# Two-layer YOCO trunk on one core: the spread of the sums of squares as two words, two of its places moved into a unit, and a cut of lower words around the last x tile

## What is computed

```python
h = h + 0.5 * swiglu(rmsnorm(h, ffn1_norm[l]), ffn1_w_gate_up[l], ffn1_w_down[l])
u = rmsnorm(h, mix_norm[l])
# layer 0: main = gated DeltaNet, projections u @ gdn_w_in; layer 1: main = forgetting attention
h = h + jnp.concatenate([main, mem_out], axis=-1) @ w_out[l]
h = h + 0.5 * swiglu(rmsnorm(h, ffn2_norm[l]), ffn2_w_gate_up[l], ffn2_w_down[l])
# after layer 0: shared_fox_kv(h) = rmsnorm(h, kv_norm) @ kv_w
```

```python
y = x32 * lax.rsqrt(jnp.mean(x32 * x32, axis=-1, keepdims=True) + EPS)   # then * gain
```

## Time and profile before

| | us |
|---|---|
| median of 3 runs (1984.55 to 1986.69) | 1986.46 |
| the profiled execution, own time | 1986.4 |
| its span, first to last instruction | 1984.7 |
| TensorE busy in it | 1959.9 |
| VectorE busy | 908.2 |
| ScalarE busy | 732.2 |
| GpSimd busy | 395.1 |

### The profile page before, as it was taken

The page is one execution under the profiler, slowest core; times in us unless marked ns, Lnnn a source line. Parts: engine busy times, 40 slices in busy tenths (PEclk is TensorE's granted clock), DMA queues, the critical chain, the costliest instruction groups (busy, mean ns, idle before and its releaser), DMA issues.

```text
span 1984.7 us, 24949 instructions
## 1 busy us (share of the span) xinstructions
PE 1959.9 (99%) x9755; PEld 1612.3 (81%) x9755; DVE 908.2 (46%) x898; ACT 732.2 (37%) x882; POOL 395.1 (20%) x274
## 2 busy tenths in 40 slices
PE   9999999999999999999999999999999999999997
PEld 7888888888777888888888888888887788888886
DVE  5544334378875543433334434343446553433323
ACT  5422222245445443432232434332235444433221
POOL 1312221113813321211110122121101041212111
PEclk9999999999999999999999999999999999999999
DMA  6243322354311333332334333323260133333232
GB/s 193 87 126 106 106 73 88 105 157 114 90 46 44 87 104 106 87 97 87 88 99 160 114 105 85 106 78 96 87 216 22 43 106 106 89 101 92 81 95 71
DMA packets 330145, 195.60 MB, mean 99 GB/s; under 512 B 18591, under 2 KB 326960, under 8 KB 329570
## 3 DMA queue, kind: packets, MB, share of 16 engines
q1 hardware_dynamic: 327248, 182.55, 32.1%
q10 hardware_dynamic: 1938, 9.00, 1.3%
q0 software_dynamic: 896, 3.16, 0.4%
HBM read 188.23 MB, written 6.46 MB: 98 GB/s over the span
## 4 chain that ended last, share of the span: by engine, by line
PE 92%; DVE 5%; ACT 2%; issue 1%; ACTq 0%; POOL 0%; DVEq 0%
PE ps L595 29%; PE ps L597 29%; PE ps L596 29%; DVE w_lo L1724 1%; DVE v L2029 1%; ACT w_hi L1269 1%; DVE q L2029 1%; PE ps L1162 1%; PE ps L1188 0%; PE ps L654 0%; PE ps L676 0%; PE ps L666 0%; PE ps L1173 0%; PE ps L903 0%; PE ps L883 0%
## 5 line engine op out<-in xcount | busy, mean ns | idle before, releaser
L595 PE MATMUL ps<-x_hi,w_hi 128*128 128x512 f32 x1792 | 707.2, 395 | 1.7 <-DVE w_lo L1724 1.6
L597 PE MATMUL ps<-x_hi,w_lo 128*128 128x512 f32 x1792 | 697.8, 389 | 0.0
L596 PE MATMUL ps<-x_lo,w_hi 128*128 128x512 f32 x1792 | 697.6, 389 | 0.0
L1269 ACT ACTIVATE w_hi<-raw 128x2048 fp32r<-128x2048 f32 (+1 forms) x186 | 320.5, 1723 | 755.7 <-PE ps L597 755.7
L1724 DVE TENSOR_TENSOR w_lo<-raw,w_hi 128x2048 fp32r<-128x2048 f32 (+1 forms) x186 | 405.9, 2182 | 208.2 <-ACT w_hi L1269 208.2
L595 PEld LDWEIGHTS ps<-x_hi,w_hi 128*128 128x128 f32 x1792 | 336.5, 188 | 76.1 <-issue 4.1
L597 PEld LDWEIGHTS ps<-x_hi,w_lo 128*128 128x128 f32 x1792 | 336.3, 188 | 70.6
L596 PEld LDWEIGHTS ps<-x_lo,w_hi 128*128 128x128 f32 x1792 | 336.6, 188 | 68.0 <-issue 1.0
L597 PE MATMUL ps<-hid_hi,w_lo 128*128 128x512 f32 x704 | 273.9, 389 | 0.0
L595 PE MATMUL ps<-hid_hi,w_hi 128*128 128x512 f32 x704 | 273.9, 389 | 0.0
L596 PE MATMUL ps<-hid_lo,w_hi 128*128 128x512 f32 x704 | 273.9, 389 | 0.0
(11 more groups left out here) (315 smaller groups left out, 1439.3 us busy)
## 6 DMA issues: line engine op xcount, KB each, us to landing
raw<-in_ffn_w_gate_up SPq DMA_DIRECT2D x174, 512.0 KB, 4.9
raw<-in_ffn_w_down SPq DMA_DIRECT2D x64, 384.0 KB, 4.0
raw<-in_ffn_w_down SPq DMA_DIRECT2D x64, 320.0 KB, 3.3
raw<-in_gdn_w_in SPq DMA_DIRECT2D x26, 512.0 KB, 4.8
raw<-in_w_out SPq DMA_DIRECT2D x16, 512.0 KB, 4.3
raw<-in_kv_w SPq DMA_DIRECT2D x12, 512.0 KB, 4.7
raw<-in_mem_w_kv SPq DMA_DIRECT2D x8, 512.0 KB, 4.2
raw<-in_fox_w_in SPq DMA_DIRECT2D x8, 512.0 KB, 4.5
```

Source lines behind the costliest of these rows:

```text
L595: nc.tensor.matmul(dst, hi, xh, start=first, stop=False)
L596: nc.tensor.matmul(dst, hi, xl, start=False, stop=False)
L597: return nc.tensor.matmul(dst, lo, xh, start=False, stop=last)
L1269: nc.scalar.activation(w_hi[s][:, 0:n], raw[s][:, 0:n], ACT.Copy).then_inc(hi_ready, 1)
```

## The change

Four edits.

1. `spread_sum` is two fp32r matmuls, ones by `sum_hi` and ones by `sum_lo`, in place of one float32 matmul. ScalarE makes `sum_hi` from `square_sum` (in `root_mean_square`, ahead of the wait for the spread), VectorE makes `sum_lo` (in `reciprocal_of_rms`, ahead of the wait for the root). The spread waits for both words (`sum_words`) and no longer for GpSimd's last add. The final phase calls the ScalarE helper too, so `sum_hi` is also made there, and nothing reads it.
2. In gdnin0 and kv0 the spread no longer stands between unit 0 and unit 1, but inside unit 1, behind its third x tile (`SPREAD_BESIDE = 2`), that is behind 18 of its 48 matmuls. In up1, foxin0 and up3 it stays between the units.
3. At the end of down0, down1 and down2 the lower words of the next phase's unit 1 are made in two halves, one ahead of the last `x_lo` and one behind it.
4. The two words of the sum take place in `gate_up`, in the half that holds the up outputs.

```diff
+SPREAD_BESIDE = 2
...
+        sum_hi = place("sum_hi", [P, SEQ], F32R, at=pair_at + 2048)
+        sum_lo = place("sum_lo", [P, SEQ], F32R, at=pair_at + 6144)
...
             def spread_sum(name, tokens=SEQ):
 
-                pe.wait_ge(sum_ready, KT * (sums_before[name] + 1))
-                nc.tensor.matmul(ps[:, 4, 0:tokens], ones[:], square_sum[:, 0:tokens],
-                                 start=True, stop=True).then_inc(sum_done, 1)
+                pe.wait_ge(sum_words, 2 * sums_before[name])
+                nc.tensor.matmul(ps[:, 4, 0:tokens], ones[:].bitcast(F32R), sum_hi[:, 0:tokens], start=True, stop=False)
+                nc.tensor.matmul(ps[:, 4, 0:tokens], ones[:].bitcast(F32R), sum_lo[:, 0:tokens],
+                                 start=False, stop=True).then_inc(sum_done, 1)
...
                     def beside(n, s):
 
+                        if n == 1 and s == SPREAD_BESIDE:
+                            spread_sum(fed_by[name])
...
                              beside=lambda c: beside(n, c))
-                        if n == 0:
-                            spread_sum(fed_by[name])
...
                 elif kind == "kv":
+                    def spread_beside(c):
+
+                        if c == SPREAD_BESIDE:
+                            spread_sum(fed_by[name])
+
                     for n in range(1 + HEADS):
...
-                             release=n == HEADS)
-                        if n == 0:
-                            spread_sum(fed_by[name])
+                             release=n == HEADS, beside=spread_beside if n == 1 else None)
...
             def root_mean_square(name, dst, tokens=SEQ):
+                act.wait_ge(sum_ready, KT * (sums_before[name] + 1))
+                nc.scalar.activation(sum_hi[:], square_sum[:], ACT.Copy).then_inc(sum_words, 1)
                 act.wait_ge(sum_done, sums_before[name] + 1)
...
             def reciprocal_of_rms(name, dst):
                 n = sums_before[name] + 1
+                dve.wait_ge(sum_words, 2 * sums_before[name] - 1)
+                nc.vector.tensor_tensor(sum_lo[:], square_sum[:], sum_hi[:].bitcast(F32), ALU.subtract).then_inc(sum_words, 1)
...
+                        if m == KT - 1 and name != last_update:
+                            cut_lo_part(u + 2 * m + 3, 0)
+                            feed_lo(name, x_lo[:, c:c + 1, :], h[:, c:c + 1, :],
+                                    gains[:, gain + c:gain + c + 1], x_hi[:, c:c + 1, :], m)
+                            cut_lo_part(u + 2 * m + 3, 1)
+                            return
```

More of the change, by code:

```diff
@@ L371, in build_trunk @@
         sq_ready, sum_zero, sum_ready = sem("sq_ready"), sem("sum_zero"), sem("sum_ready")
-        sum_done = sem("sum_done")
+        sum_done, sum_words = sem("sum_done"), sem("sum_words")
         rms_ready, rstd_ready = sem("rms_ready"), sem("rstd_ready")
```

## The result

| | before | changed |
|---|---|---|
| median, us | 1986.36 | 1993.13 |
| lowest to highest of 7 runs | 1984.55 to 1986.69 | 1991.37 to 1994.61 |
| profiled execution, own time | 1986.4 | 1991.37 |
| its span | 1984.7 | 1989.6 |

The ratio is 1.0034, with a 95% interval of 1.0025 to 1.0043: slower, by 6.8 us at the median and by 4.9 in the profiled executions' spans. The forecast was 1991.8, with a range from 1988.8 to 1994.3.

The account below looks back on a forecast made before the run. TensorE, busy 1959.9 of 1984.7 us, was taken to bound the kernel. The terms 4.7 + 1.5 - 0.4 - 0.2 - 0.2 = +5.4 us on the profiled 1986.4 gave 1991.8 us, range 1988.8 to 1994.3.

Parts of the forecast that it names:

- The delay of the root, 4.82: In gdnin0 and kv0, the spread inside unit 1 makes the root start 4.82 us later, with everything hanging on it.
- gdnin0 +4.7: In gdnin0, TensorE waits 1.6 us ahead of unit 2 and 2.9 ahead of unit 3; phase 4.7 us late.
- the 0.28 us of slack ahead of unit 3: In gdnin0, unit 3's lower words are ready only 0.28 us before TensorE needs them: all the chain's slack.
- The first rival: Waits inside VectorE's and ScalarE's chain are slack and swallow the root's delay: 1985.5 us; chance 10%.
- kv0 +1.5: In kv0, unit 2 starts 1.4 us later, plus 0.1 for starting again; no wait ahead of unit 3.
- foxin0 -0.4: In foxin0, the words have time, so the cheaper spread gains 0.4 us.
- up3 -0.2: In up3, the words come late as in up1, leaving a gain of 0.2 us.
- up1 -0.2: In up1, a 0.15 us wait for late words and 0.05 restart cut the spread's 0.40 us gain to 0.2.
- The final phase, 0: In the final phase, the copy and table load fit into ScalarE's 4.31 us wait for products, costing 0.
- From there late by the same amount, and I count no more: After gdnin0's unit 3, TensorE and VectorE stay late by the same amount; nothing further counted.
- the third rival: The clock falls in gdnin0's new 2.9 us wait, costing 2.3 us more: 1994.1 us; chance 10%.
- the second rival: Later in gdnin0, TensorE's 2.7 us of waits for turned values shrink, giving back loss: 1989.1 us; chance 13%.

Follow-up runs that it names:

- experiment 5: Changed kernel with the spread behind the first x tile of unit 1 in place of the third: 1987.43 us, ratio 1.0006.
- experiment 6: Changed kernel with the spread behind the second x tile of unit 1 in place of the third: 1990.68 us, ratio 1.0022.
- experiment 12: Changed kernel with the spread behind the fifth x tile of unit 1 in place of the third: 1999.38 us, ratio 1.0066.
- experiment 7: Changed kernel with unit 1's banks emptied and unit 3's lower words made earlier in gdnin0's gate chain: 1989.98 us, ratio 1.0018.
- experiment 8: Changed kernel with two words only in up1, foxin0 and up3, float32 spread between units in gdnin0 and kv0, halves kept: 1986.24 us, ratio 0.9999.
- experiment 3: Kernel before with only unit 1's lower words made in two halves around the last x_lo: 1986.70 us, ratio 0.9998.
- experiment 11: Changed kernel with the spread back between the units in gdnin0 alone: 1988.24 us, ratio 1.0007.
- experiment 10: Changed kernel measured and profiled a second time, no edit: 1991.38 us, ratio 1.0029.
- experiment 9: Kernel before with two words in up1, foxin0 and up3, and gdnin0's first query scaling behind the third v_tok copy: 1985.25 us, ratio 0.9994.

## Why the prediction was right

**The delay of the root, 4.82: measured 4.76.** It was built from the place of the 18th matmul, the end of the halves and the length of two matmuls. The halves ended at 404.19 + 2.31 = 406.50, less the offset of 0.25 at 406.25, predicted 406.3: the second half took 2.31 us where the first took 1.23, so the add did cost 1.1, as assumed.

**gdnin0 +4.7: measured 4.5** at unit 3's start (433.54 - 428.77 - 0.25). The two waits are 1.47 and 2.68, predicted 1.6 and 2.9. The whole step rested on the 0.28 us of slack ahead of unit 3, and on reading the 3.36 us ahead of the gate step as part of the chain. Both held: the chain is late by one amount from the root to unit 3. The first rival, that the chain has slack, is dead: experiments 5, 6 and 12 move the root by steps and the time follows. Experiments 1 and 4 show that it is the place and not the words: the move alone costs +9.6 us, words and halves without it +1.0. The words without halves cost +3.7 (experiment 2), with three falls of the clock in the profile.

**kv0 +1.5: measured +1.48** in the table of lateness (1.24 us of wait, the rest restart and boundary). **foxin0 -0.4: -0.40. up3 -0.2: -0.23 (5.17 to 4.94). up1 -0.2: -0.21 (4.47 to 4.26)**, each from the last start of upper words ahead of the spread to the first behind it. Up1's spread in the changed kernel (timeline of TensorE):

```profile
688.42 0.50 PE L649 MATMUL ps<-sum_hi,ones 128*128 128x512 f32 x1
688.76 0.39 PE L650 MATMUL ps<-sum_lo,ones 128*128 128x512 f32 x1
688.99 0.40 PE L598 MATMUL ps<-x_hi,w_hi 128*128 128x512 f32 x1
```

From the spread's start to the next dense matmul pass 0.57 us, where the float32 spread cost 0.85; the 0.50 instead of 0.39 in the first row is the mark of a stop just before, here for sum_lo, which VectorE ends at 688.37 (687.68 + 0.69), 0.05 us ahead of that row.

**The final phase, 0.** The copy and the table load fit into the wait for the last add's products, as read from the earlier trace rows: ScalarE still waits 2.31 us ahead of the root, 4.31 before.

```profile
1981.37 0.26 ACT L1297 ACTIVATE small<-ps,eps 128x4 f32<-128x4 f32 x1 [2.31 <-PE ps L1251]
```

**"From there late by the same amount, and I count no more": this step failed**, twice, and the two misses cancel in the profiled execution. One: the third rival came true once behind the wait of 2.68 us and costs 1.3 us; the prediction had priced it at 2.3 and at one chance in ten, and the profiles of experiments 1, 2, 6, 7, 8 and 12 have falls too. Two: the second rival came true in part. The lateness falls by 1.6 us at the turned values, though not because what they wait for did not move. The rows fit a meeting on the SBUF port. Timelines of VectorE and GpSimd of the kernel before (start us, us long):

```profile
537.42 2.83 DVE L2062 TENSOR_TENSOR q<-q,exp_g 128x1024 f32<-128x1024 f32 x1
...
537.15 2.01 POOL L2471 COPY tri_t<-tri 96x1024 f32<-96x1024 f32 x1
```

The same two timelines of the changed kernel:

```profile
543.43 1.23 DVE L2079 TENSOR_TENSOR q<-q,exp_g 128x1024 f32<-128x1024 f32 x1
...
543.49 3.07 POOL L2488 COPY tri_t<-tri 96x1024 f32<-96x1024 f32 x1
```

Whichever comes second waits for the other. Before, GpSimd came first by 0.27 us, and VectorE's product took 2.83 us; in the changed kernel VectorE came first by 0.06 us, took 1.23, and GpSimd's copy grew from 2.01 to 3.07. The second ends behind the first by about what it takes alone: 1.09 us for the product (540.25 against 539.16), 1.90 for the copy (546.56 against 544.66). It is no work of the change: experiment 3, where the spread has not moved, has it too, and its profile is 1.5 us early from there on. TensorE's wait for turned values goes with it: 1.1 to 1.4 us in the profiles where VectorE won (the changed kernel's two, experiments 2, 3 and 12), 2.6 to 2.7 where it did not (experiments 1, 4 to 8, 11).

So the predicted 1991.8 stood 1.3 below the first median and 0.4 above the second. With the offset at down0's end, the fall and the meeting taken out, the two profiles of the changed kernel are 5.0 and 5.1 us late at their ends, where the sum said 5.4: that part is borne out by rows. That the median came so near is in part luck, since neither miss was counted and both profiles are of the faster executions. A slip in the prediction's own bounds: 1.3 us worse in each of two places gives 1994.4, not 1994.2. The timed runs of the changed kernel reach from 1989.6 to 1995.3 over both sessions, a width of 5.7 over 13 runs; the kernel before reaches from 1984.4 to 1989.0 over its 88, 4.6, in three groups: 8 up to 1985.1, 65 from 1985.8 to 1987.0, 15 from 1987.7 on. The distance of the groups is near the 1.6 us of a fall or of a meeting. That clock falls and port meetings make this width is what the profiles suggest; no profile exists of each timed run, so it is argued, not shown. Open too is why the same wait brings a fall in one execution and none in another.

## What to carry to other kernels

A step that is moved "beside" dense work keeps everything that hangs on it waiting. Follow what is computed from its result to the last user that feeds the busy engine, and read the slack there (here 0.28 us, where the shares of busy time were 46% and 37%); a move longer than that slack cost the difference in full here (4.76 us of delay, 0.28 of slack, 4.5 lost). An idle time inside a chain is slack only if the other engine's step that ends it does not hang on the moved step too. And a wait can have a price beyond its length: behind waits of 1.86 us and more the matmuls sometimes ran at half clock.

## What the runs showed of the hardware

**The clock falls in mid-kernel, and not in every execution.** Behind waits of TensorE the granted clock went to 0.50 (1.2 GHz) for some 3 us, once for at least 6 (experiment 12, 422 to 428), with matmuls 0.43 us apart instead of 0.227. Behind unit 3's wait and the one for g_lo a fall cost 1.3 to 1.6 us; the long one of experiment 12 delayed nothing further, since unit 3's lower words were as late in any case. Behind the wait of 1.86 us for g_lo it fell in the profiles of experiments 2, 6, 7 and 8 and in none of the other ten; behind the two of 1.9 us for sum_lo it fell both times in experiment 2; behind the one of 2.67 or 2.68 us it fell in two profiles of four; behind 4.19 and 4.0 both times. Behind waits of 1.83 us and less for another engine none showed in mid-kernel. The Trainium skill (TensorE: Matmul & The Clock Gate, Part 1) has TensorE drop from 2.4 to 1.2 GHz after being idle long enough. The rows agree that idleness comes first and that the two levels are these; that the same wait has two outcomes is this case's to add.

**Meetings of VectorE and GpSimd cost 1.1 us or 1.6, and a small shift turns them.** q's product took 1.23 us where it began 0.04 to 0.06 ahead of GpSimd's copy and 2.8 where it began 0.26 or 0.27 behind. x_lo of 128x512 took 0.75 us or 1.87, the add beside it 1.85 or 1.29; the long x_lo stands in gdnin0 in the profiles of experiments 3 to 6, 8, 10 and 11, in kv0 or foxin0 in others too. Which of the two will wait can't be read from the starts there: the add begins 0.04 us behind x_lo in the changed kernel and in experiment 3 alike, with opposite outcomes. The Trainium skill's rule of a port taken for a whole instruction (SBUF — State Buffer, section "SBUF: two separate sides") agrees with the lengths in both. In a kernel with such meetings, a shift of all engines by some tenths can change the time by more than a small edit does, such as those of experiments 3, 8 and 9.
